# Expert weights on two queues instead of one: GpSimd issues the down weights, SyncE the gate/up weights

## The reference

```python
def moe_ffn(h, router_w, router_b, w_gu, b_gu, w_down, b_down):
    t = h.reshape(n, d)                                  # 256 x 1024
    logits = (t @ router_w + router_b).astype(jnp.float32)
    top_val, top_idx = lax.top_k(logits, TOP_K)          # 4 of 32
    gates = jax.nn.softmax(top_val, axis=-1)
    ...
    def expert_block(args):
        xe, eid = args
        gu = xe @ w_gu[eid] + b_gu[eid]                  # w_gu[eid]: 1024 x 2048
        g, u = jnp.split(gu, 2, axis=-1)
        g = jnp.minimum(g, SWIGLU_LIMIT)
        u = jnp.clip(u, -SWIGLU_LIMIT, SWIGLU_LIMIT)
        act = (u + 1.0) * (g * jax.nn.sigmoid(SWIGLU_ALPHA * g))
        return act @ w_down[eid] + b_down[eid]           # w_down[eid]: 1024 x 1024
    ...
    out = jax.ops.segment_sum(y, slot_tok, num_segments=n + 1)[:n]
```

## Time and profile before

| | us |
|---|---|
| median of 3 runs | 1445.78 (1444.41 to 1447.06) |
| the profiled execution | 1443.56 |
| its span, first to last instruction | 1441.5 |
| TensorE busy | 1340.4 (93%) |
| VectorE, ScalarE, GpSimd busy | 436.8, 228.7, 15.1 |
| DMA | 477.74 MB, mean 331 GB/s |

### The profile page before, as it was taken

One profiled execution on the slowest core, in us unless ns is written; L12 is line 12 of the kernel. 1 busy time (PEld: TensorE's weight loads), 2 busy tenths in 40 slices (PEclk: granted clock), 3 DMA queues, 4 the chain that ended last, 5 costly groups with the idle time before them and its releaser, 6 DMA issues.

```text
span 1441.5 us, 17010 instructions
## 1 busy us (share of the span) xinstructions
PE 1340.4 (93%) x6088; PEld 610.8 (42%) x6089; DVE 436.8 (30%) x909; ACT 228.7 (16%) x411; POOL 15.1 (1%) x47
## 2 busy tenths in 40 slices
PE   4999999999997999999999999999999976799997
PEld 2866865877853333333332233333333322233332
DVE  1001333222223233333333233233333322232433
ACT  3001223776011010010011000010010000000101
POOL 0000000111000000000000000000000000000000
PEclk9999999999996999999999999999999999999999
DMA  9747566312855999999999999999999997479994
GB/s 366 258 136 264 185 232 233 105 72 86 327 216 222 394 415 417 416 419 418 418 417 416 418 418 419 414 418 417 416 419 419 418 417 325 154 310 419 419 418 188
DMA packets 100899, 477.74 MB, mean 331 GB/s; under 512 B 8435, under 2 KB 9020, under 8 KB 65020
## 3 DMA queue, kind: packets, MB, share of 16 engines
q1 hardware_dynamic: 100580, 476.12, 82.5%
q10 hardware_dynamic: 280, 1.05, 0.2%
HBM read 476.09 MB, written 1.05 MB: 331 GB/s over the span
## 4 chain that ended last, share of the span: by engine, by line
PE 79%; DMA 10%; SPq 6%; issue 2%; DVE 1%; ACT 1%; DVEq 0%; ACTq 0%
PE bank L1390 26%; PE bank L1422 12%; PE bank L1138 12%; DMA down_ring<-in_w_down 7%; PE bank L1236 4%; PE bank L1129 4%; PE bank L1349 4%; PE bank L1379 4%; PE bank L1357 3%; SPq L367 3%; SPq L362 2%; PE bank L1297 2%; DMA gu_ring<-in_w_gu 2%; DMA gu_ring<-in_w_ada 1%; PE bank L1083 1%
## 5 line engine op out<-in xcount | busy, mean ns | idle before, releaser
L1390 PE MATMUL bank<-gu_ring,scratch 128*64 128x512 f32 x2048 | 466.2, 602 | 22.2 <-issue 19.8
L1390 PEld LDWEIGHTS bank<-gu_ring,scratch 128*64 128x64 f32 x2048 | 143.9, 138 | 311.9 <-issue 306.3
L1422 PE MATMUL bank<-down_ring,scratch 128*64 128x512 f32 x1024 | 231.0, 597 | 9.9 <-DMA down_ring<-in_w_down 9.9
L1138 PE MATMUL bank<-gu_ring 128*128 128x256 f32 x768 | 173.3, 384 | 2.1 <-ACT gu_ring L528 2.1
L1138 PEld LDWEIGHTS bank<-gu_ring 128*128 128x128 f32 x768 | 145.1, 192 | 27.2 <-issue 7.9
L636 ACT ACTIVATE scratch<-bank 128x512 f32<-128x512 f32 x32 | 19.1, 598 | 739.6 <-PE bank L1390 739.6
L1422 PEld LDWEIGHTS bank<-down_ring,scratch 128*64 128x64 f32 x1024 | 69.0, 136 | 149.0 <-issue 122.0
L969 DVE TENSOR_TENSOR scratch<-bank,bgu 128x512 f32<-128x512 f32 x32 | 22.1, 692 | 280.6 <-PE bank L1357 280.6
L951 DVE TENSOR_TENSOR xres<-xres,bank 128x512 f32<-128x512 f32 x132 | 81.9, 683 | 51.5 <-PE bank L1379 51.5
L1357 PE MATMUL bank<-ident,scratch 128*128 128x128 f32 x400 | 65.8, 288 | 24.6 <-ACT scratch L632 22.7
L1357 PEld LDWEIGHTS bank<-ident,scratch 128*128 128x128 f32 x400 | 42.2, 141 | 106.7 <-ACT scratch L632 51.1
(11 more groups left out here) (249 smaller groups left out, 813.9 us busy)
## 6 DMA issues: line engine op xcount, KB each, us to landing
gu_ring<-in_w_gu SPq DMA_DIRECT2D x256, 1024.0 KB, 20.0
down_ring<-in_w_down SPq DMA_DIRECT2D x128, 1024.0 KB, 16.3
gu_ring<-in_w_in SPq DMA_DIRECT2D x32, 1024.0 KB, 7.9
gu_ring<-in_w_ada SPq DMA_DIRECT2D x20, 1024.0 KB, 8.9
down_ring<-in_w_ada SPq DMA_DIRECT2D x4, 1024.0 KB, 10.3
gu_ring<-in_w_pa SPq DMA_DIRECT2D x4, 1024.0 KB, 6.3
gu_ring<-in_w_pb SPq DMA_DIRECT2D x4, 1024.0 KB, 6.4
gu_ring<-in_w_o SPq DMA_DIRECT2D x4, 1024.0 KB, 10.0
```

The costliest lines, as they stand in the source:

```text
L1138: last = M(dst[:, b * T:(b + 1) * T], group_chunk(group, kt // 4)[:, kt % 4, cols], hT[:, kt, :], start=kt == 0, stop=kt == KT - 1)
L1390: last = M(bank[f // 2][64 * a:64 * a + 64, :], xT[:, kt % 4, kt // 4, :], gu_ring[:, 8 * half + kt, f * 512:(f + 1) * 512], start=kt == 0 ...
L1422: last = M(bank[7][64 * a:64 * a + 64, :], act_sb[:, kt % 4, kt // 4, :], down_ring[:, kt // 2, (kt % 2) * D + a * 512:(kt % 2) * D + (a + ...
```

## The change

GpSimd issues every transfer of the down weights on a queue of its own, behind its last mask. SyncE keeps gate/up and all else, and the switch of order at expert 16 is gone. Each queue refills its own ring as that ring's slots come free.

```diff
--- before.py
+++ after.py
@@ -57,7 +57,6 @@
 CAP = 64
 BLOCKS = T // CAP
 PAIRS = NE // 2
-TOGETHER = NE // 2
 
 
 R_C, R_N1, R_N2, R_ADA, R_SUB, R_LQ, R_LK, R_END = 0, 8, 16, 24, 72, 73, 74, 75
@@ -363,11 +362,6 @@
                              w_gu[0, bass.ds(expert, 1), kt * P:(kt + 1) * P, :].rearrange("a p n -> p (a n)")
                              ).then_inc(slot_in[8 * half + kt], 16)
 
-            def load_down(expert, j):
-                sp.dma_start(down_ring[:, j, :].rearrange("p (k n) -> p k n", k=2),
-                             w_down[0, bass.ds(expert, 1), j * 2 * P:(j + 1) * 2 * P, :]
-                             .rearrange("a (k p) n -> p (a k) n", p=P)).then_inc(down_in[j], 16)
-
             for kt in range(KT):
                 sp.dma_start(ada_chunk(kt), w_ada[0, kt * P:(kt + 1) * P, 0:ADA_COLS]).then_inc(ada_in[kt], 16)
 
@@ -383,8 +377,6 @@
                     for half in range(2):
                         sp.dma_start(y_sb[64 * half:64 * half + NE, :], b_down[0, :, half * 512:(half + 1) * 512]
                                      ).then_inc(bdown_in, 16)
-                    for j in range(4):
-                        load_down(0, j)
                     for kt in range(2):
                         load_gu(1, 1, kt)
                 if n >= 4:
@@ -421,27 +413,11 @@
                     sp.wait_ge(gu_used, item * 8 + (kt - 15))
                     load_gu(item, half, kt)
 
-            def load_item_down(item):
-                for j in range(4):
-                    sp.wait_ge(down_used, item * 4 + (j - 3))
-                    load_down(item, j)
-
-
-
             load_item_gu(2, 0)
-            load_item_down(1)
-            with sp.Fori(1, TOGETHER // 2) as n:
+            with sp.Fori(1, PAIRS - 1) as n:
                 load_item_gu(n * 2 + 1, 1)
-                load_item_down(n * 2)
                 load_item_gu(n * 2 + 2, 0)
-                load_item_down(n * 2 + 1)
-            load_item_down(TOGETHER)
-            load_item_gu(TOGETHER + 1, 1)
-            load_item_down(TOGETHER + 1)
-            with sp.Fori(TOGETHER // 2 + 1, PAIRS) as n:
-                for half in range(2):
-                    load_item_gu(n * 2 + half, half)
-                    load_item_down(n * 2 + half)
+            load_item_gu(NE - 1, 1)
             sp.wait_ge(taken_done, NE + 1)
             sp.dma_start(fgb, final_g.partition_broadcast(P)).then_inc(fg_in, 16)
             for tt in range(TT):
@@ -488,6 +464,19 @@
                 if s >= 2:
                     pool.wait_ge(sbw_ready, s - 1)
                     causal(sb_a[:, (s - 2) % 3, :]).then_inc(sbw_masked, 1)
+
+            def load_down(expert, j):
+                pool.dma_start(down_ring[:, j, :].rearrange("p (k n) -> p k n", k=2),
+                               w_down[0, bass.ds(expert, 1), j * 2 * P:(j + 1) * 2 * P, :]
+                               .rearrange("a (k p) n -> p (a k) n", p=P)).then_inc(down_in[j], 16)
+
+            pool.wait_ge(sbpv_done, SBH)
+            for j in range(4):
+                load_down(0, j)
+            with pool.Fori(1, NE) as item:
+                for j in range(4):
+                    pool.wait_ge(down_used, item * 4 + (j - 3))
+                    load_down(item, j)
 
 
         @block.scalar
```

## The result

The changed kernel takes 1475.76 us (median of 4 runs, 1466.37 to 1475.99); the kernel before, timed beside it, 1445.39. The ratio is 1.0193, with a 95% interval from 1.0152 to 1.0234: slower by 28 us (the two medians stand 30 apart). The forecast was 1469.7 us with its own range from 1462 to 1478. The profiled execution took 1475.80 us (span 1474.1).

The account below looks back on a forecast made before the run. Late weights on full DMA queues were taken to bound the kernel up to expert 24; 22 experts at 29.85 us add 26.1 to 1443.6, the rest 0, giving 1469.7 us, own range 1462 to 1478 (wider 1444 to 1486).

Parts of the forecast that it names:

- What bounds, and where it counts: DMA full from 544 to 1169 us, 30.2 us per expert against TensorE's 27.88; only time up to expert 24's end is open.
- SyncE's wait and the early start cost or give nothing: SyncE no longer waiting for down_used (371.9 us) and first four down transfers moved to GpSimd: each costed at 0.
- Turns of one packet: Two DMA queues alternate single packets, so 4 KB down rows get a third of bytes; four down transfers take 29.6 to 30.1 us.
- The working with completion packets: If small completion packets take turns too, a down transfer takes 7.25 us, about 7.4 with their own time, 29.6 for four.
- The down queue never runs empty again: Once TensorE waits for the last down slot, freed slots keep GpSimd's queue filled; loop pace is four down transfers, 29.6 to 30.1 us.
- the lock: State where TensorE waits for the last down slot and the down queue stays at its share, 29.6 to 30.1 us per expert.
- 29.85 us per expert: Pace taken for 22 experts from expert 2's end: expert 24's down product ends at 1200.5 us, +26.1.
- The 269.2 us behind it stay: From expert 24's down product to the end of execution, 269.2 us left unchanged, with up to 16 MiB of gate/up already there.
- B: In the expert loop down gets half or more, gate/up is late instead: +10.2 us, 1453.7 us or 1450; chance 0.21.
- C: GpSimd's queue moves fewer bytes per us, slowing the whole stretch: 6.6 us per percent, 1483 at 2 percent; chance 0.12.
- D: Mixed rate of 424 GB/s holds in the loop and down is not starved: 1436 us; chance 0.12.
- E: Nothing moves: in the loop, sharing cost and faster rate cancel, +3.3 to -1.4 us, 1442 to 1447 us; chance 0.08.

Follow-up runs that it names:

- second profile: The changed kernel run once more, unchanged, and profiled again: 1472.75 us, ratio 1.0180 to the kernel before.

## Why the prediction held, step by step

**What bounds, and where it counts.** Right. The transfers are full from 544 us to expert 24's end, at 418 GB/s, and the end of expert 24's down product carries 24.4 of the 32.2 us. Of the signs named, down takes 20.2 us to land at the median of the expert shown, and at experts 3 to 24 gate/up lies 10 to 13 transfers ahead. From expert 2's end (543.02) to expert 24's, 655.7 - 613.4 = 42.3 us were lost, where the prediction had some 43.

**SyncE's wait and the early start cost or give nothing.** Right as far as the gain goes. Gate/up now runs at 201 GB/s in the window 1240:1268, where the earlier trace rows had 10 between 1220 and 1248, and nothing was gained by it. What the freed queue costs behind expert 24 stands in the last step below.

**Turns of one packet.** Right, and shown by four kernels that differ in who issues or in row size: landings 7.25 us apart for 4 KB against 8 KB rows on GpSimd's queue and 7.3 on ScalarE's, 5.1 for 4 against 4, 5.0 for 8 against 8. The working with completion packets had 7.25 us and then added a little for their own time; that addition was too much, and the plain 7.25 fits. The Trainium skill ("DMA: Bandwidth & Descriptors", section "Queues, rings and completion order") says that an engine drains a whole packet, typically 9 to 17 descriptors, before it switches rings. The runs do not agree, on the software queue either. The spacings alone would not tell, since any equal number of records in turn gives the same ones. The first 2 us in which GpSimd's records stand beside SyncE's again, 1107:1109 of the changed kernel, do (q1 is SyncE's queue, q0 GpSimd's; records, MB, share):

```profile
q1 hardware_dynamic: 70, 0.55, 65.9%
q0 software_dynamic: 73, 0.30, 37.1%
```

With nine in turn, each of the 16 engines would have sent up to nine of GpSimd's 159 ns records first, some 144 in those 2 us (an estimate from the 159 ns).

**The down queue never runs empty again.** This step failed. If it held, the pace would be four times 7.25, 29.0 us per expert; measured from one expert's last down landing to the next's, experts 5 to 24 average 29.8. The pace alternates between about 29 and about 30 us, with 31.8 and 31.7 where TensorE's clock had fallen at 1015.6 and 1077.0. GpSimd's issues from 1103 to 1131 us (start, us, what; in brackets the idle time before) show why:

```profile
1103.04 0.71 POOL L469 DMA_DIRECT2D down_ring<-in_w_down  x1 [22.97 <-PE bank L1411]
1104.84 0.71 POOL L469 DMA_DIRECT2D down_ring<-in_w_down  x1 [1.09 <-PE bank L1411]
1106.47 0.71 POOL L469 DMA_DIRECT2D down_ring<-in_w_down  x1 [0.91 <-PE bank L1411]
1108.18 0.71 POOL L469 DMA_DIRECT2D down_ring<-in_w_down  x1 [1.00 <-PE bank L1411]
1130.92 0.71 POOL L469 DMA_DIRECT2D down_ring<-in_w_down  x1 [22.03 <-PE bank L1411]
```

The transfer issued at 1108.18 lands at 1136.65; the next expert's first was issued at 1130.92, 5.7 us before: no gap, and the next four end at 1139.30 + 26.25 = 1165.55, 28.9 us later. One expert earlier it is otherwise. The first row's issue, at 1103.04, came when the transfers before it were nearly through: the last of them landed at 1105.0. From issue to landing beside a full gate/up queue pass 11.8 us, of which 7.25 are the transfer, so an issue must come 4.6 us before the last landing to follow without a gap. This one came 1.9 before; it landed at 1114.9, 9.9 us after the last one instead of 7.25, and the queue was empty between: from 1105.1 to 1106.5 us the engines have no record of it, only SyncE's:

```profile
q1 hardware_dynamic: 86, 0.59, 101.2%
```

The term of the prediction that was too small is the 2.4 us from an issue to the start of its transfer, read on an idle queue; beside a full one it is these 4.6.

Such a gap makes the next last landing late, TensorE waits in the last quarter (1108.18 + 28.47), and then the slots that it has freed before have been queued long enough; the expert behind it waits less (0.8 us instead of 3.0) and frees its first slot late again. So experts alternate. Where the clock has not fallen the issue comes 3.4 to 3.8 us ahead and the gap is 0.9 to 1.4 us.

This is also where GpSimd's 0.4 us of latency, its later issue (0.66 against 0.17 us) and the clock enter, and why taking GpSimd's extra latency as hidden by the lock, "so 0", was off. On ScalarE's queue the pace is 29.1 us, near four turns; the first issue comes at least 4.0 us ahead of the last landing, and the clock does not fall between 494 and 1190 us. GpSimd's queue and the clock drops were taken away together there, so of the 11.5 us between the two at expert 24 the runs do not tell how much is either's. The Trainium skill ("DMA: Bandwidth & Descriptors", section "Specifications") gives the first byte after about 1 us on a software queue against about 0.6 on a hardware queue; the 0.4 us between first landings, busy (11.8 and 11.4) and on an idle queue (5.3 us here, 4.9 in the earlier trace rows), agrees with that difference.

**29.85 us per expert.** Right in sum, by luck, since two errors cancel: it took 29.6 to 30.1 for turns alone, which are 29.0, and nothing for the gaps, which are 0.8. Expert 24's down product ends 1.8 us before the forecast's 1200.5 in this profile, and 5.5 behind it in the second one.

**The 269.2 us behind it stay.** This step failed, by 7.9 us, more than the whole miss of the profiled execution, 6.1. In the second profile it is 272.0 us (1477.93 - 1205.96), 2.8 too many, and most of the miss lies ahead of expert 24's end instead. The second block of tokens takes 49.15 us instead of 46.85, with the clock at 0.51 for its first 17 us (the window 1196:1213 above). Then the lock comes back where the prediction had excluded it, "with up to 16 MiB of gate/up already there". From the chain:

```profile
1277.58 8.58 issue
...
1373.61 28.56 DMA down_ring<-in_w_down
...
1402.22 3.68 PE bank L1411 x8
1405.90 4.61 PE bank L1379 x16
```

The last down transfer of expert 29 lands 28.56 us after its issue; TensorE's matmuls stand still for 3.1 us, and those behind run at the lower clock (8 in 3.68 us, where 1.96 is usual). The down product takes 5.1 us more than its 7.0 by both together, and the 16 matmuls behind it 4.61 us instead of 3.43. Full gate/up slots do not help: from 1328 to 1402 us the down landings within experts 27 to 29 are 6.0 to 7.4 us apart again, since SyncE, which no longer waits for down_used, loads gate/up ahead of them and takes two thirds of the bytes. In the second profile the stop is 2.0 us, with no fall of the clock. The prediction's aside that two more experts at the locked pace would cost 4 us had the order of size. The 9.71 us of the earlier trace rows before expert 26 are 8.58 now: a gain of 1.1.

**The rivals.** B did not occur in the change, but does with equal rows, at its price. C and D are refuted by 418 GB/s, E by the interval.

## What to carry to other kernels

Where the transfer engines are full, a second queue adds no bandwidth; it only changes the order of the bytes, and its share goes by the size of its packets and not by who needs them first. Keep one queue in the order of need, or give the urgent queue the larger rows; and before holding the other queue back, ask what will keep the engines busy meanwhile. Rows of 8 KB in place of 4 KB, on the one queue, made this kernel 0.42% faster [0.23%, 0.61%].

## What the hardware showed unexpected

- TensorE's granted clock goes down to its 1.2 GHz level at five of the nine stalls of 2.0 to 3.1 us in the down product: in the profile after at 896, 1015.6, 1077.0, 1196.5 and 1401.3 us, for 3.4 us in the first three, 17.1 at 1196.5 and 6.8 at 1401.3. Eight matmuls take 2.70 to 3.68 us then, not 1.96. In the kernel before there is none between 459.5 and 1183 us. So a wait for weights can cost more than its length, and it then frees the slot later as well. What decides between the five and the four the rows do not tell: at one stall of 3.0 us the clock stayed, at one of 2.1 it fell.
- Rows of 8 KB move at 422 GB/s and rows of 4 KB in the same stream at 417; with gate/up in 4 KB rows too it is 410.
- The small packets that report a transfer's end take turns like the data: without them the spacing would be 16 x (159 + 311) ns = 7.5 us, with them 7.25. The count agrees: from 1143 to 1165 us of the changed kernel the two queues send almost equal numbers with the small ones, but 1664 - 926 = 738 of 8 KB and 926 - 158 = 768 of 4 KB:

```profile
DMA packets 1664, 9.19 MB, mean 418 GB/s; under 512 B 158, under 2 KB 158, under 8 KB 926
q1 hardware_dynamic: 834, 6.05, 66.1%
q0 software_dynamic: 830, 3.15, 35.7%
```
